# Recurrence of an RWKV-7 mixer: the next pair's scores around this pair's chunk terms, a second matrix tile, turns and head sums inside the levels, one key scaling on GpSimd

## The chip, the cores and the metric

The kernel runs on one core of one Trainium2 chip. The metric is the device time of one execution in microseconds (us), the median of three runs for the kernel before.

## The reference, cut to what matters

The program is two transformer-like blocks on 512 tokens of width 1024, all in float32. The change lies in the second block's RWKV-7 time mixer. For each of 8 heads (64 channels each) and each token it computes

```
state = state * w_t + (state @ a_t) b_t^T + v_t k_t^T      # a = -kk, b = kk * a, decay w
y_t   = state @ r_t
```

and after it a group norm, a bonus `sum(r*k*r_k) * v` and a gate. Everything ahead of it (first block, attention, projections) and behind it (merge, convolutional feed-forward) is not touched.

## The kernel before, in words

**Chunks and pairs.** The recurrence is rewritten in chunks of 64 tokens (`C`), 8 chunks. Heads are taken two at a time: pair m = 0 to 3, 128 channels on 128 partitions. For a pair, keys and removal keys scaled by the running decay ("hats") are multiplied with each other per chunk and head (`rw_scores`, line 973), which gives small 64x64 matrices `mats`; a triangular system of 64x64 is inverted by doubling in levels k = 1 to 5; the inverse is applied (`ug`, line 1126), and the terms of each chunk follow (lines 1137 to 1152: the map of the state and the outputs it adds). After all four pairs a short walk over the 8 chunks (lines 1163 to 1189) chains them.

**Halves.** All eight 64x64 units of a pair are split into two halves of two token tiles each, `half` 0 and 1. Half 0 uses PSUM banks 4 and 5, half 1 banks 0 and 1 (`HALF_BANKS`), and banks 2 and 3 take their transposed copies (`TURN_BANKS`). So while half 0 waits for a copy, TensorE works on half 1.

**One pair on TensorE** (line 1085 on), in program order: wait for the five hats; scores of half 0; turns of the keys from channels to tokens by transposes (`rw_turn(m, 0)`, banks 6 and 7); scores of half 1; turn of the values (`rw_turn(m, 1)`) and of the removal keys (`rw_turn_a`); `level_start(0)`; the two sums over heads of the next pair (`head_sums`, lines 957 and 960: of the squared keys and of the bonus product); then the levels. A level is `level_x` of half 0, `level_dt` of half 1 of the level before, `level_x` of half 1, `level_d` 0, `level_dt` 0, `level_d` 1. The first has `level_start(1)` in it and after its `level_x` 1 `keyed_values` (line 1037) into banks 2 and 3, whose copy `akv_read` must be over before `level_dt`. Then come `ug` of both halves, the wait for their copies, and the chunk terms into banks 0 to 3.

**The other engines** follow the same order, each a fixed list with waits on semaphores. ScalarE (line 1609 on) copies the turned keys, `Dm` and half of the `DT` copies out of PSUM, takes the exponentials of the decays (`decays`), the norm of the keys (`key_norm`) and the key rates of the pair after next (`key_rates`), and copies `UG` and half of the chunk terms. VectorE (line 2190 on) masks the scores into `mats`, makes the level starts, adds the identity in `X`, makes the other `DT` copies, and prepares the next pair inside the levels: `sums_out`, `decay_sum` (a scan), `decayed` (two products, line 2147 and 2149, `MOD * INV` being the scaling of the keys), `removal`, then `replacement` and `keys`. It reads the other half of the chunk terms (lines 2231 and 2232). GpSimd (line 501 on) makes the level masks `OT` (line 509), one product of the next pair (`rate_over_decay`, line 492) and `fold_decay` (line 498).

**Order between pairs.** `mats` is one tile and the scores of pair m+1 share banks 0, 1, 4 and 5 with pair m, so pair m+1's scores stand behind pair m's chunk terms, half 1 also behind their reading. "Hats" counts five operations per pair.

## Time and profile before

| | us |
|---|---|
| median of 3 runs (lowest, highest) | 1942.52 (1942.04, 1943.04) |
| the profiled execution: its own time | 1942.0 |
| its span, first to last instruction | 1940.1 |
| scores of pair 0 to the next pair's scores | 1334.8 to 1363.4 |
| pair 1 | 1363.4 to 1391.25 |
| pair 2 | 1391.25 to 1419.3 |
| pair 3, to the last chunk term | 1419.3 to 1447.0 |

TensorE is busy 95% of the span, with weight loads of 75%, VectorE 40%, ScalarE 22%, GpSimd 65%. Two thirds of the program are large 128x512 products; the four pairs take 112 us of 1940, in thousands of 64x64 products. In a row of the timeline the first number is the start, the second how long the group lasts, and square brackets hold the idle time before it and what ended it. A product's recorded duration includes its passage through the array, so neighbouring rows overlap: what one group costs its engine is the distance from its start to the next start.

### The profile page before, as it was taken

To read this page: it belongs to the slowest core of one execution; us is meant where nothing else is said; L and a number is where in the kernel's file an instruction comes from. 1 tells how busy PE (TensorE), PEld (TensorE's weight loads), DVE (VectorE), ACT (ScalarE), POOL (GpSimd) and SP (SyncE) were. 2 spreads that over 40 slices of the span, in tenths; PEclk is the share of its full clock that TensorE was granted. 3 is DMA by queue.
4 is the path that set the end of the run, shared out by engine and by line. 5 is a ranking of instruction groups with operands and counts; after the bars stand their busy time and mean duration, and the time that the engine had idled before them with its cause. 6 is when DMAs were issued, how large, how long until landed. Compare 5 with 4: busy or idle time off the path is not lost.

```text
span 1940.1 us, 29759 instructions
## 1 busy us (share of the span) xinstructions
PE 1843.9 (95%) x11700; PEld 1463.9 (75%) x11700; DVE 774.7 (40%) x1348; ACT 436.0 (22%) x885; POOL 1269.6 (65%) x621
## 2 busy tenths in 40 slices
PE   7999999988779999999899999998889999999998
PEld 5888888856557888888577787667776878888887
DVE  4333361164654333311322434515755445555301
ACT  3000001033522000000212245644534122112000
POOL 6888888844075888888566643242465867777773
PEclk8999999989989999999899999999999999999999
DMA  4222333221021222233332352140014322222331
GB/s 156 94 93 96 103 91 98 83 92 66 12 87 59 94 96 97 93 99 96 137 131 76 121 180 70 55 153 34 4 42 196 98 87 96 93 95 92 101 92 60
DMA packets 58779, 180.32 MB, mean 93 GB/s; under 512 B 6931, under 2 KB 13843, under 8 KB 58172
## 3 DMA queue, kind: packets, MB, share of 16 engines
q1 hardware_dynamic: 49132, 165.83, 25.4%
q10 hardware_dynamic: 9552, 13.13, 2.0%
q8 instruction: 72, 1.18, 0.2%
q14 instruction: 23, 0.19, 0.0%
HBM read 165.81 MB, written 13.13 MB: 92 GB/s over the span
## 4 chain that ended last, share of the span: by engine, by line
PE 89%; DVE 7%; ACT 2%; issue 1%; DMA 0%; SPq 0%; DVEq 0%; ACTq 0%
PE bank L546 26%; PE bank L547 25%; PE bank L548 25%; PE bank L596 1%; PE bank L893 1%; PE bank L922 1%; PE bank L866 1%; DVE h_lo L1714 1%; PE bank L828 1%; DVE xT L1761 1%; DVE tmp L1758 1%; PE bank L1081 1%; PE bank L1053 0%; PE bank L647 0%; DMA prm<-params_dram 0%
## 5 line engine op out<-in xcount | busy, mean ns | idle before, releaser
L454 POOL TENSOR_TENSOR w_hi<-w_raw,one 128x1024 fp32r<-128x1024 f32 (+1 forms) x279 | 524.5, 1880 | 537.9 <-PE bank L548 527.5
L456 POOL TENSOR_TENSOR w_lo<-w_raw,w_hi 128x1024 fp32r<-128x1024 f32 (+1 forms) x279 | 691.8, 2480 | 21.9
L546 PE MATMUL bank<-h_hi,w_hi 128*128 128x512 f32 x1528 | 621.1, 406 | 26.8 <-DVE h_lo L1714 12.1
L547 PE MATMUL bank<-h_lo,w_hi 128*128 128x512 f32 x1528 | 598.9, 392 | 0.0
L548 PE MATMUL bank<-h_hi,w_lo 128*128 128x512 f32 x1528 | 598.3, 392 | 0.0
L546 PEld LDWEIGHTS bank<-h_hi,w_hi 128*128 128x128 f32 x1528 | 289.2, 189 | 109.8 <-issue 28.3
L547 PEld LDWEIGHTS bank<-h_lo,w_hi 128*128 128x128 f32 x1528 | 289.5, 189 | 68.0 <-issue 10.7
L548 PEld LDWEIGHTS bank<-h_hi,w_lo 128*128 128x128 f32 x1528 | 289.1, 189 | 61.2
L546 PE MATMUL bank<-a_hi,w_hi 128*128 128x512 f32 x528 | 205.4, 389 | 0.0
L547 PE MATMUL bank<-a_lo,w_hi 128*128 128x512 f32 x528 | 205.4, 389 | 0.0
L548 PE MATMUL bank<-a_hi,w_lo 128*128 128x512 f32 x528 | 205.4, 389 | 0.0
L1294 ACT ACTIVATE tmp<-tmp 128x512 f32<-128x512 f32 x44 | 27.9, 633 | 426.6 <-DVE tmp L1725 426.6
L546 PEld LDWEIGHTS bank<-a_hi,w_hi 128*128 128x128 f32 x528 | 99.1, 188 | 20.6
L548 PEld LDWEIGHTS bank<-a_hi,w_lo 128*128 128x128 f32 x528 | 99.1, 188 | 20.6
L547 PEld LDWEIGHTS bank<-a_lo,w_hi 128*128 128x128 f32 x528 | 99.1, 188 | 20.5
L1751 DVE TENSOR_TENSOR acc<-acc,sq 128x512 f32<-128x512 f32 x16 | 29.6, 1848 | 189.3 <-ACT sq L1303 189.3
L1725 DVE TENSOR_TENSOR tmp<-bank,rstd 128x512 f32<-128x512 f32 x44 | 30.4, 692 | 132.4 <-PE bank L548 123.8
L1733 DVE TENSOR_TENSOR a_hi<-tmp,bank 128x512 f32 x44 | 30.3, 688 | 132.2 <-PE bank L548 132.2
L509 POOL TENSOR_TENSOR OT<-mats,rcs 128x256 f32<-128x256 f32 x40 | 32.5, 827 | 69.6 <-DVE mats L2195 61.9
L1687 ACT ACTIVATE tmp<-bank,prm 128x512 f32<-128x512 f32 x44 | 34.3, 780 | 147.8 <-DVE bank L2326 147.8
L1728 DVE TENSOR_TENSOR tmp<-tmp,rstd 128x512 f32<-128x512 f32 x44 | 47.1, 1071 | 31.4 <-ACT tmp L1294 31.4
L596 PE MATMUL bank<-sq,cst 128*128 128x512 f32 x96 | 55.1, 679 | 3.8 <-ACT sq L1268 3.8
(347 smaller groups left out, 1944.9 us busy)
## 6 DMA issues: line engine op xcount, KB each, us to landing
w_raw<-w_ffn_gu_dram SPq DMA_DIRECT2D x88, 512.0 KB, 3.4
w_raw<-w_conv_up_dram SPq DMA_DIRECT2D x44, 512.0 KB, 3.5
w_raw<-w_ffn_down_dram SPq DMA_DIRECT2D x32, 448.0 KB, 3.2
w_raw<-w_ffn_down_dram SPq DMA_DIRECT2D x16, 512.0 KB, 3.5
w_raw<-w_out_dram SPq DMA_DIRECT2D x16, 512.0 KB, 3.5
w_raw<-w_gates_dram SPq DMA_DIRECT2D x16, 512.0 KB, 3.5
w_raw<-w_rwkv_dram SPq DMA_DIRECT2D x14, 512.0 KB, 3.5
w_raw<-w_conv_down_dram SPq DMA_DIRECT2D x16, 448.0 KB, 3.3
```

The costliest lines, as they stand in the source:

```text
L454: nc.gpsimd.tensor_tensor(w_hi[:, s, 0:width], raw, one[:, 0:1].to_broadcast([P, width]), ALU.mult).then_inc(sem("w_rounded"), 1)
L456: nc.gpsimd.tensor_tensor(w_lo[:, s, 0:width], raw, w_hi[:, s, 0:width].bitcast(F32), ALU.subtract).then_inc(sem("w_split"), 1)
L509: nc.gpsimd.tensor_tensor(OT[:, k % 2, units_of(half), :] .rearrange("p (n e) t -> p n e t", e=2), mats[:, 2 * half:2 * half + 2, :, 0, :] ...
L546: nc.tensor.matmul(dst, hi, rhs_hi[:, k, :], start=start and k == k0, stop=False)
L547: nc.tensor.matmul(dst, hi, rhs_lo[:, k, :], start=False, stop=False)
L548: last = nc.tensor.matmul(dst, lo, rhs_hi[:, k, :], start=False, stop=stop and k == k1 - 1)
L596: nc.tensor.matmul(bank[b][:, :], ones, sq[:, k % 2, :], start=(k == 0), stop=(k == n - 1)).then_inc(sem(used), 1)
L1687: nc.scalar.activation(tmp[:, v, :], bank[2 * u + v][:, :], ACT.Identity, bias=bias, scale=w)\
L1725: nc.vector.tensor_tensor(tmp[:, u, :], bank[2 * u][:, :], rstd[:, :], ALU.mult)\
L1728: nc.vector.tensor_tensor(tmp[:, u, :], tmp[:, u, :], rstd[:, :], ALU.mult)\
L1733: nc.vector.tensor_tensor(hi, tmp[:, u, :], bank[2 * u + 1][:, :], ALU.mult)\
L1751: nc.vector.tensor_tensor(acc[:, :], acc[:, :], sq[:, m % 2, :], ALU.add).then_inc(sem(tag + "_acc"), 1)
```

## The change

The diff below is cut; names as above. `pe`, `act`, `dve`, `pool` are TensorE, ScalarE, VectorE and GpSimd.

```diff
+            odd_mats = in_h("mats1", [P, NT, 2, 4, C])
-        HALF_BANKS, TURN_BANKS = ((4, 5), (0, 1)), (2, 3)
+        HALF_BANKS, TURN_BANKS, SCORE_BANKS = ((4, 5), (0, 1)), (2, 3), ((4, 5), (6, 7))
-            mats = in_a("mats", [P, NT, 2, 4, C])
+            pair_mats = [in_a("mats", [P, NT, 2, 4, C]), odd_mats]
 # pool
+            def key_over_decay(m):
+                MOD = pair_sets[m % 2][1]
+                pool.wait_ge(*nth("decays", 2 * (m + 1)))
+                pool.wait_ge(*nth("rk_product", m + 1))
+                nc.gpsimd.tensor_tensor(MOD[:, :], MOD[:, :], INV[:, :], ALU.mult).then_inc(sem("hats"), 1)
                     if k == 4 and m < 3:
                         rate_over_decay(m + 1)
+                    if k == 5 and m < 3:
+                        key_over_decay(m + 1)
 # pe
             def keyed_values(m):
-                pe.wait_ge(*nth("rw_tok", 4 * m + 3))
-                pe.wait_ge(*nth("d_ready", 10 * m + 2))
+                pe.wait_ge(*nth("rw_tok", 4 * m + 4))
+                if m < 3:
+                    pe.wait_ge(*nth("bonus_done", m + 2))
...                                              # its banks are 6 and 7, not 2 and 3
             def level_dt(m, k, half):
-                if k == 1:
-                    pe.wait_ge(*nth("akv_read", m + 1))
-                elif k == 5:
+                if k == 5:
+            pe.wait_ge(*nth("hats", 5))
+            rw_scores(0, 0)
+            rw_turn(0, 0)
+            pe.wait_ge(*nth("rw_tok", 2))
+            rw_scores(0, 1)
             for m in range(4):
-                pe.wait_ge(*nth("hats", 5 * (m + 1)))
-                rw_scores(m, 0)
-                rw_turn(m, 0)
-                if m:
-                    pe.wait_ge(*nth("chunk_terms_read", m))
-                rw_scores(m, 1)
-                rw_turn(m, 1)
-                rw_turn_a(m)
                 if m:
                     pe.wait_ge(*nth("chunk_terms_copied", m))
                 level_start(m, 0)
-                if m < 3:
-                    pe.wait_ge(*nth("rw_tok", 4 * m + 4))
-                    head_sums(m + 1)
                 for k in range(1, 6):
                     level_x(m, k, 0)
                     if k > 1:
                         level_dt(m, k - 1, 1)
                     else:
+                        if m:
+                            pe.wait_ge(*nth("chunk_terms_read", m))
                         level_start(m, 1)
+                        rw_turn(m, 1)
                     level_x(m, k, 1)
                     if k == 1:
+                        rw_turn_a(m)
+                    elif k == 2 and m < 3:
+                        pe.wait_ge(*nth("rw_tok", 4 * m + 3))
+                        square_sum(m + 1)
+                    elif k == 3 and m < 3:
+                        pe.wait_ge(*nth("rw_tok", 4 * m + 4))
+                        bonus_sum(m + 1)
+                    elif k == 4:
                         keyed_values(m)
...
+                pe.wait_ge(*nth("akv_read", m + 1))
...                                              # ug of both halves
+                if m < 3:
+                    pe.wait_ge(*nth("hats", 5 * (m + 2)))
+                    pe.wait_ge(*nth("ug_read", 2 * m + 1))
+                    rw_scores(m + 1, 0)
+                    rw_turn(m + 1, 0)
                 pe.wait_ge(*nth("ug_read", 2 * m + 2))
...                                              # chunk terms of pair m
+                if m < 3:
+                    pe.wait_ge(*nth("rw_tok", 4 * m + 6))
+                    rw_scores(m + 1, 1)
 # act, inside the levels
-                    if k == 1 and m < 3:
-                        key_norm(m + 1)
+                    if k == 1:
+                        rw_turned(m, 2)
+                        rw_turned(m, 3)
                     elif k == 2 and m < 3:
                         decays(m + 1)
-                    elif k == 4 and m < 2:
-                        key_rates(m + 2)
+                    elif k == 3 and m < 3:
+                        key_norm(m + 1)
+                    elif k == 4:
+                        act.wait_ge(*nth("akv", m + 1))
+                        nc.scalar.activation(AtV[...], two_banks(6, 4 * C), ACT.Copy).then_inc(sem("akv_read"), 1)
+                        if m < 2:
+                            key_rates(m + 2)
...                                              # UG copies of both halves
+                if m < 3:
+                    rw_turned(m + 1, 0)
+                    rw_turned(m + 1, 1)
 # dve
-                nc.vector.tensor_tensor(MOD[:, :], MOD[:, :], INV[:, :], ALU.mult).then_inc(sem("hats"), 1)
+                if m == 0:
+                    nc.vector.tensor_tensor(MOD[:, :], MOD[:, :], INV[:, :], ALU.mult).then_inc(sem("hats"), 1)
+            masked_scores(0, 0)
+            masked_scores(0, 1)
             for m in range(4):
...                                              # the masking of both halves stood here
-                    if m < 3 and k < 5:
-                        (sums_out, decay_sum, decayed, removal)[k - 1](m + 1)
-                level_dt_out(m, 5)
+                    if m < 3 and k == 1:
+                        decay_sum(m + 1)
+                    elif m < 3 and k == 2:
+                        square_sum_out(m + 1)
+                    elif m < 3 and k == 3:
+                        decayed(m + 1)
+                        bonus_out(m + 1)
+                    elif m < 3 and k == 4:
+                        removal(m + 1)
                 if m < 3:
                     replacement(m + 1)
+                level_dt_out(m, 5)
                 if m < 2:
                     keys(m + 2)
+                if m < 3:
+                    masked_scores(m + 1, 0)
                 dve.wait_ge(*nth("chunk_terms", m + 1))
...                                              # the two readings of the chunk terms
+                if m < 3:
+                    masked_scores(m + 1, 1)
```

`masked_scores(m, half)` is the masking and level start that stood at the head of VectorE's loop, `square_sum` and `bonus_sum` are the two halves of `head_sums`, `square_sum_out` and `bonus_out` those of `sums_out`. `mats` of odd pairs lies in `odd_mats`, and scores of half 1 now go to banks 6 and 7.

## Rows read from the trace of the kernel before

**Rows 1.** The page's chain that ended last, shares of the span.
```profile
PE 89%; DVE 7%; ACT 2%; issue 1%; DMA 0%; SPq 0%; DVEq 0%; ACTq 0%
```

**Rows 2.** Windows, one row per pair: stretch, its us, busy us by engine, TensorE clock.
```profile
1334.80:1363.40 28.60, 24.13 (x874) 20.43 (x878) 20.57 (x36) 14.52 (x32) 9.95 (x11) 1.00 0.04 13
1363.40:1391.25 27.85, 23.87 (x899) 20.31 (x894) 20.41 (x36) 14.29 (x32) 11.60 (x13) 1.00 0.02 5
1391.25:1419.30 28.05, 23.89 (x892) 20.23 (x887) 18.96 (x34) 12.98 (x30) 11.60 (x13) 1.00 0.01 4
1419.30:1447.00 27.70, 23.66 (x891) 21.15 (x883) 12.41 (x25) 11.20 (x26) 20.59 (x18) 0.94 0.02 5
```

**Rows 3.** Waits in the four pairs: who for whom, total us, times, longest.
```profile
PE bank L1066 <- DVE X L2213: 3.7, 3, 1.2
PE bank L1081 <- ACT AtV L1621: 1.7, 4, 0.5
```

**Rows 4.** Timeline of TensorE, pair 2; the last row is pair 0's.
```profile
1391.25 0.40 PE L982 MATMUL bank<-AR,KK 64*64 64x128 f32 x8
...
1393.26 0.45 PE L982 MATMUL bank<-AR,KK 64*64 64x128 f32 x8
...
1394.88 1.15 PE L1008 MATMUL bank<-rcs,AR 64*64 64x64 f32 x32
...
1396.72 1.12 PE L957 MATMUL bank<-sq,rcs 128*128 128x512 f32 x2
...
1398.64 0.46 PE L1053 MATMUL bank<-Dm,OT 64*64 64x64 f32 x16
1398.92 0.34 PE L1020 MATMUL bank<-rcs,DT 64*64 64x64 f32 x6
...
1400.67 0.46 PE L1053 MATMUL bank<-Dm,OT 64*64 64x64 f32 x16 [0.88 <-ACT DT L1618]
...
1403.00 0.45 PE L1053 MATMUL bank<-Dm,OT 64*64 64x64 f32 x15
...
1414.05 1.36 PE L1126 MATMUL bank<-AtV,DT 64*64 64x128 f32 x32
1416.13 0.34 PE L1137 MATMUL bank<-mats,UG 64*64 64x64 f32 x8 [0.72 <-ACT UG L1644]
...
1347.29 0.45 PE L1053 MATMUL bank<-Dm,OT 64*64 64x64 f32 x15
```

**Rows 5.** Timeline of VectorE and ScalarE, start of pair 2.
```profile
1391.50 0.69 DVE L2231 TENSOR_TENSOR pin<-bank,AR 128x512 f32<-128x512 f32 x1 [2.34 <-PE bank L1152]
...
1392.82 1.29 DVE L2195 TENSOR_TENSOR mats<-bank,rstd 128x512 f32<-128x512 f32 x2
...
1394.60 0.83 DVE L2207 TENSOR_TENSOR DT<-X,rcs 128x256 f32<-128x256 f32 x1
...
1391.99 0.59 ACT L1651 ACTIVATE pin<-bank 128x512 f32<-128x512 f32 x1
```

**Rows 6.** One product alone (line view), and two on both engines at once.
```profile
L2128 DVE TENSOR_TENSOR MOD<-MOD,pin x4: 693/693/693, 1312.4 to 1387.7; 128x512 f32<-128x512 f32 x4
...
1408.18 1.76 DVE L2149 TENSOR_TENSOR MOD<-MOD,CUM 128x512 f32<-128x512 f32 x1
...
1407.62 1.78 POOL L492 TENSOR_TENSOR sig<-sig,CUM 128x512 f32<-128x512 f32 x1 [2.48 <-ACT CUM L1574]
```

**Rows 7.** Timeline of TensorE in pair 3, then two windows there.
```profile
1427.97 0.65 PE L1053 MATMUL bank<-Dm,OT 64*64 64x64 f32 x16 [0.88 <-ACT DT L1618]
...
1431.36 0.30 PE L1053 MATMUL bank<-Dm,OT 64*64 64x64 f32 x2
...
1441.12 0.33 PE L1126 MATMUL bank<-AtV,DT 64*64 64x128 f32 x2
...
1424.80:1428.00 3.20, 1.43 (x54) 1.19 (x53) 1.68 (x3) 1.32 (x4) 3.13 (x4) 1.00 0.02 5
1428.00:1431.40 3.40, 3.13 (x97) 2.94 (x100) 0.42 (x1) 0.94 (x3) 2.44 (x4) 0.51 0.00 0
```

More of the change, by code:

```diff
@@ L510, in _ @@
                                                 .rearrange("p (n e) t -> p n e t", e=2),
-                                                mats[:, 2 * half:2 * half + 2, :, 0, :],
+                                                pair_mats[m % 2][:, 2 * half:2 * half + 2, :, 0, :],
                                                 level[k].unsqueeze(1).unsqueeze(1).to_broadcast([P, 2, 2, C]),
@@ L952, in lora, with square_sum @@
                     .then_inc(sem("lora"), 1)
[L954 removed]
+            def square_sum(m):
                 pe.wait_ge(*nth("rw_square", m + 1))
@@ L958, in head_sums, with bonus_sum @@
                     .then_inc(sem("rw_head_sum"), 1)
+            def bonus_sum(m):
                 pe.wait_ge(*nth("rk_product", m + 1))
@@ L969, in _ @@
             fill(1)
-            head_sums(0)
+            square_sum(0)
+            bonus_sum(0)
             fill(3)
@@ L981, in rw_scores @@
                             rows, tok = half_rows(e), slice(n * P + c * C, n * P + c * C + C)
-                            last = nc.tensor.matmul(bank[HALF_BANKS[half][e]][half_rows(c), at], src[rows, tok],
+                            last = nc.tensor.matmul(bank[SCORE_BANKS[half][e]][half_rows(c), at], src[rows, tok],
                                                     AR[rows, n, :, half_rows(c)], start=True, stop=True,
@@ L1036, in keyed_values @@
                         rows = half_rows(c)
-                        last = nc.tensor.matmul(bank[2 + c][half_rows(e), n * C:n * C + C], mats[rows, n, e, 2, :],
+                        last = nc.tensor.matmul(bank[6 + c][half_rows(e), n * C:n * C + C], mats[rows, n, e, 2, :],
                                                 Vt[rows, n, half_rows(e)], start=True, stop=True,
@@ L1608, in _ @@
             by_bank = lambda x: x.rearrange("p (n b) t -> p b n t", b=2)
+            rw_turned(0, 0)
+            rw_turned(0, 1)
             for m in range(4):
                 AtV = pair_sets[m % 2][3]
-                for i in range(4):
-                    rw_turned(m, i)
                 for half in range(2):
@@ L2119, in decay_sum @@
                 dve.wait_ge(*nth("lora_read", m + 1))
+                if m:
+                    dve.wait_ge(*nth("hats", 5 * m))
                 nc.vector.tensor_tensor_scan(CUM[:, :], reset[:, :], SG[m], 0.0, ALU.mult, ALU.add)\
@@ L2166, in replacement @@
                 nc.vector.tensor_copy(PC[:, m, 1:], decay[:, 0:NCH - 1, C]).then_inc(sem("hats"), 1)
-                dve.wait_ge(*nth("hats", 5 * (m + 1)))
             def level_dt_out(m, k):
@@ L2183, in _ @@
             decayed(0)
-            sums_out(0)
+            square_sum_out(0)
+            bonus_out(0)
             removal(0)
@@ L2189, in _, with masked_scores @@
             dve.wait_ge(*nth("fill_late", 16 * LATE))
+            def masked_scores(m, half):
+                mats = pair_mats[m % 2]
+                dve.wait_ge(*nth("rw_scores", 2 * m + half + 1))
+                for e in range(2):
+                    last = nc.vector.tensor_tensor(mats[:, 2 * half:2 * half + 2, e, :, :],
+                                                   bank[SCORE_BANKS[half][e]][:, :]
+                                                   .rearrange("p (n j t) -> p n j t", n=2, j=4),
+                                                   mask4[:, :].rearrange("p (n j t) -> p n j t", n=2, j=4),
+                                                   ALU.mult)
+                last.then_inc(sem("mats_ready"), 1)
+                dve.wait_ge(*nth("mats_ready", 2 * m + half + 1))
+                to = X[:, units_of(half), :]
+                link(nc.vector.tensor_tensor(to.rearrange("p (n e) t -> p n e t", e=2),
+                                             mats[:, 2 * half:2 * half + 2, :, 0, :],
+                                             level[0].unsqueeze(1).unsqueeze(1).to_broadcast([P, 2, 2, C]),
+                                             ALU.mult))
+                nc.vector.tensor_tensor(DT[:, units_of(half), :], to,
+                                        eye2.unsqueeze(1).to_broadcast([P, 4, C]), ALU.add)\
+                    .then_inc(sem("level_start"), 1)
```

36 lines of the change are left out of this document (9 added, 27 removed).

## The prediction

> **What bounds the kernel now.** I read the page's chain first: TensorE holds 89% of it, so this is a TensorE-bound program [rows 1], and the change touches only the four pairs of the recurrence. Then one window per pair [rows 2]: each takes about 28 us, TensorE works 23.7 to 24.1 of them, and no other engine is busy for more than 20.6. Nothing is saturated but TensorE, and it idles about 4 us per pair. All the change can win by filling is those 4 us, some 16 us of 1942 over four pairs, 0.8%; it removes no product of TensorE's and adds none. Third, where the idle time lies: in the waits, TensorE stands three times for `X` of VectorE (up to 1.2 us each, total 3.7, one in each of pairs 0 to 2, where VectorE scales the keys ahead of `X` in level 4) and 0.5 for the copy of the keyed values [rows 3]. In the timeline of pair 2 there is 0.88 ahead of level 1's second half and 0.72 for the copy of `UG` [rows 4]. These four make 3.3 of the 4.2 us that pair 2 idles.
>
> I cut a pair into three parts and measure each from pair 2, T being the moment when the last chunk term of the pair before has left TensorE (1391.25): head, from T to level 2 (1403.00), 11.75 us; levels, from there to `ug` (1414.05), 11.05; tail, from there to the next T (1419.30), 5.25 [rows 2, 4]. They add to 28.05.
>
> **The head after the change.** Scores of half 0 and the key turns have moved out of it: 1391.25 to 1393.26, 2.0 us [rows 4]. So have the head sums, 1396.72 to 1398.64, 1.9 us, and the keyed values. But now the head is no longer filled by them and VectorE sets it. It reads the chunk terms from T+0.25 and is free for the second half's masking at T+1.57; masking, `X` and `DT` take from 1392.82 to 1395.43, 2.6 us [rows 5], and half 1's masking must stand behind the reading. So `level_start(1)` can go at T+4.25. From a level start to the `level_x` that reads its copies, pair 2 shows 1398.92 to 1400.67, 1.75 us [rows 4], so `level_x` 1 of half 1 goes at T+6.0. Half 0 is earlier: ScalarE's copies of the chunk terms end at T+1.33 [rows 5], so its start goes at T+1.5, its `level_x` at T+3.25. The turn of the values lies in the gap before T+6.0 and costs nothing; without that cover it would cost 0.6. From `level_x` of half 1 to level 2 pair 2 takes 1400.67 to 1403.00, 2.33 [rows 4]; the keyed values (about 0.5) and the wait for their copy (0.5) go out, and the turn of the removal keys (1.0; 1.15 with its last product's passage) comes in: 2.35. Level 2 begins at T+8.35 instead of T+11.75, a gain of 3.4. What is late next there is VectorE, not TensorE.
>
> **The levels after.** The four levels 2 to 5 take 11.05 in pair 2. Pair 3, which prepares no next pair, shows what they cost TensorE with nothing in the way: 1431.36 to 1441.12, 9.76 [rows 7]. Now the two head sums (1.9) and the keyed values (0.5) stand in them, all on TensorE's own list: 9.76 + 1.9 + 0.5 = 12.2. The 1.2 us wait for `X` is gone with the key scaling, and the `keyed_values` wait too. The decays' copies, the key norm and the key rates on ScalarE lie beside TensorE's extra products, except in level 5 of pairs 0 and 1, where the copy of the keyed values stands ahead of the key rates and `DT` of level 5 behind both.
>
> What the trace doesn't show is GpSimd's key scaling at that place. It follows the masks of level 5 and falls on VectorE's `removal`, whose products read two tiles of SBUF. The nearest rows: a 128x512 product alone takes VectorE 0.69; beside GpSimd's product of the same size (1.78) it takes 1.76 [rows 6], 1.07 more. So the price lies between nothing (they miss each other, or the key rates cover it) and 1.05 on `X` of level 5. I take 0.3, nearer to the lower end because in pairs 0 and 1 the key rates hide about 0.45 of it and VectorE may be through its first product before GpSimd begins. GpSimd's own time is slack: it ends some 3 us before the hats are wanted. Levels: 12.5, a loss of 1.45.
>
> On this pair of engines the Trainium skill (GPSIMD Engine Reference, Specifications) says that GpSimd's SBUF interfaces are shared with VectorE and that instructions with two SBUF inputs contend. The row agrees: 0.69 against 1.76. By this rule alone, with every two-input product of `removal` met, the sum would take the upper end, 0.75 more in each of three pairs.
>
> **The tail after.** `ug` 0 needs its copy; today both copies are over 2.08 after `ug` begins (1414.05 to 1416.13) [rows 4], and one is some 0.6 sooner. The next pair's scores and turns, 2.0 us, go in at +1.5 and the chunk terms at +3.5 instead of +2.08: a loss of 1.4, of which the 0.72 wait has paid its part. The hats are there: `replacement` now stands before the last `DT` copy, whose product takes longer than it. The masking of half 0 (2.6) lies beside the chunk terms (3.2, 1416.13 to 1419.30). If that cover failed, it would delay the reading at T and cost what sticks out. Queued on ScalarE behind its wait for the key turns are only the chunk copies, which are wanted later.
>
> **The sum.** Pair 0: its head is short on other grounds (1334.8 to 1347.29 is 12.5 us [rows 2, 4], its scores cannot be earlier, VectorE masks both halves in a row in both kernels); only the head sums go from the second half's way, between 0 and 1 us, I take 0.5. So -0.5 + 1.45 + 1.4 = +2.35. Pairs 1 and 2: -3.4 + 1.45 + 1.4 = -0.55 each. Pair 3: no next pair, so no head sums, no key scaling and the old tail. Its head goes from 12.06 (1419.30 to 1431.36) to 8.35, -3.7, the levels gain the keyed values, +0.5: -3.2 [rows 2, 7]. Together 2.35 - 1.1 - 3.2 = -1.95.
>
> **The clock.** In pair 3 the granted clock falls from 2.4 to 1.2 GHz for 3.4 us, after a stretch in which TensorE was busy 1.43 of 3.2 us; what pair 2 does in 2.33 us (1400.67 to 1403.00) takes 3.39 there (1427.97 to 1431.36), 1.06 more [rows 4, 7]. My head has full clock. But the new head is thin in every pair: level start, `level_x`, level start and value turn, about 2.9 us of products in the 5.1 between the scores and T+6.0, near to the ratio at which it fell in pair 3; the head sums that fill this stretch now in pairs 0 to 2 are gone. The price lies between 0 and four falls at 1.06 to 1.5 (the stretch behind now holds the 1.0 us turn of the removal keys, which would double). I count one fall, 1.06, as the trace before has one. Net: -1.95 + 1.06 = -0.9.
>
> The profiled execution took 1942.0 with a span of 1940.1, half a us below the median 1942.52. 1942.0 - 0.9 = 1941.1, and with that half 1941.6. This kernel's comparison can tell 0.2%, 3.9 us, from no change: faster means below 1938.6, slower above 1946.4.
>
> **Rivals.**
> - *Slower: the clock falls in every pair.* Place: T+1 to T+6 of each head. For it: the row of pair 3, and that the change thins the very stretch. Against it: dense products (chunk terms, scores) stand just before, and 2.9 of 5.1 is more than 1.43 of 3.2. Price: 1.5 in each of four pairs, 6.0 instead of 1.06: -1.95 + 6.0 = +4.05, 1946.6. It decides from four falls on; with two or three the result is within 0.2%.
> - *Faster: my chains overstate the waits.* If the halves interleave so that a pair idles 2 us instead of 3.5 (TensorE 23.9 of 25.9), pairs 1 and 2 give -2 each and pair 0 +0.8, with pair 3's -3.2: -6.4, less one fall, 1937.2. For it: the four waits named above are all addressed. Against it: the level start behind VectorE is a new wait of some 2.3 us in each head that nothing fills.
> - *VectorE becomes the bound.* It is busy 20.4 of 28 us already [rows 2], and the reading of the chunk terms comes behind the masking of half 0. If its work shifts each T-chain by 1 us in pairs 1 to 3, +3: 1944.6. For it: nothing on VectorE overtakes. Against it: the key scaling leaves it, 0.7 to 1.8 us [rows 6].
> - *The change doesn't do what it says*, since the scores must still wait for the hats or the turned keys: the tail grows by 1 us in three pairs, also 1944.6.
>
> On the first: the Trainium skill (TensorE: Matmul & The Clock Gate, What's actually happening) says that the default is the throttled clock and activity releases it. By that rule thin heads pay in each pair, the first rival's 1946.6; pair 3's row agrees, while pairs 0 to 2, whose idle gaps lie apart, kept full clock [rows 2].
>
> **How the numbers follow.** Forecast 0.46; clock rival 0.16; faster rival 0.24; VectorE bound 0.09; hats 0.05. The first holds to within 3 us, 1938.6 to 1944.6. Faster by over 0.2%: the faster rival and a little of the forecast, 0.26. Slower: the clock rival and an edge of the others, 0.18. Within: 0.56. The range adds the faster rival's point and the slower's with 1 us: 1937.0 to 1947.5; bounds of the unknown costs alone, -1.95 - 0.9 at no collision and no fall and -1.95 + 2.25 + 6.0 at both in full, give 1939.7 to 1948.8.
>
> **What would show it.** Right: the first `level_x` of half 1 about 6 us behind the last chunk term, with TensorE idle ahead of it for VectorE's `DT`; no wait for `X` in level 4; levels 2 to 5 at 12.2 to 12.8 in pairs 0 to 2; scores about 1.5 behind `ug`; pair 0 longer than before, pairs 1 and 2 27 to 28 us, pair 3 nearer to 24.5. VectorE's product at GpSimd's key scaling of 1.7 us or 0.7 settles the collision. Wrong: pairs 1 and 2 under 26.3 or over 28.5, or a granted clock below 1 in more than two heads.

## The result, and the profile after

| | before | after |
|---|---|---|
| median of ten runs each, us (lowest, highest) | 1942.66 (1939.51, 1944.7) | 1948.99 (1945.19, 1951.6) |
| ratio after to before, 95% interval | | 1.0032 [1.0024, 1.0041] |
| profiled execution: its time, its span | 1942.0, 1940.1 | 1945.74, 1943.9 |
| the four pairs, in the profiled execution | 112.20 | 119.65 |

The change made the kernel 6.3 us slower. The forecast was 1941.6, the range ended at 1947.5. The four pairs alone are 7.45 us longer; in this one execution pair 0 began at 1331.65 instead of 1334.80, ahead of anything that was changed, which is why the spans lie only 3.8 apart. I therefore compare the pairs from here on.

The page of the kernel after; its chain answers to [rows 1]:

```profile
PE 89%; DVE 8%; ACT 2%; issue 1%; DMA 0%; SPq 0%; DVEq 0%; ACTq 0%
```

The chain says nothing: a change of 0.3% doesn't show in whole per cents. Windows of the kernel after, one per pair, columns as in [rows 2], and the four pairs as one window:

```profile
1331.65:1363.13 31.48, 27.54 (x921) 23.16 (x924) 22.63 (x39) 15.72 (x34) 11.71 (x13) 0.95 0.04 12
1363.13:1393.15 30.02, 25.36 (x891) 21.78 (x886) 20.20 (x35) 14.18 (x32) 13.28 (x14) 0.94 0.02 4
1393.15:1423.15 30.00, 25.46 (x898) 21.72 (x894) 18.92 (x33) 13.09 (x30) 13.27 (x14) 0.94 0.01 4
1423.15:1451.30 28.15, 22.62 (x851) 20.50 (x840) 9.91 (x21) 9.81 (x24) 20.77 (x17) 0.88 0.02 4
...
1331.65:1451.30 119.65, 100.98 (x3516) 87.16 (x3516) 71.66 (x128) 52.80 (x120) 59.03 (x58) 0.93 0.02 6
```

The same one window of the kernel before:

```profile
1334.80:1447.00 112.20, 95.55 (x3516) 82.11 (x3516) 72.35 (x131) 52.99 (x120) 53.75 (x55) 0.98 0.02 7
```

Read the first two numbers and the clock. Both have 3516 matmul records: the work is the same. TensorE was busy 5.4 us longer for it (95.55 to 100.98), the clock being 0.93 instead of 0.98, and idle 2.0 longer (16.65 to 18.67). Every pair has a clock below 1 now, where before only pair 3 had [rows 2].

What it idled for, from the waits of TensorE in that window (who waits for whom, us in total, times, longest); it answers to [rows 3]:

```profile
PE bank L1031 <- DVE DT L2244: 4.0, 4, 1.3
PE bank L993 <- issue: 3.5, 3, 1.4
PE bank L1065 <- ACT DT L1642: 3.5, 4, 0.9
PE bank L1091 <- issue: 2.5, 3, 1.1
PE bank L1078 <- issue: 1.5, 2, 1.2
...
PE bank L1091 <- DVE X L2255: 0.5, 1, 0.5
```

The 3.7 us of waits for `X` in front of `level_d` and the 1.7 for the keyed values are gone, as intended. In their place stands "issue", a wait for nothing the profile shows: eleven idle places, 8.35 us in the four pairs by the timeline, where the kernel before has three, 1.11 us. The waits for data fell from 15.5 to 10.3 us, and the new ones ate all of that and 2 us more.

The timeline of TensorE in pair 2, which answers to [rows 4], T being 1393.15:

```profile
1393.15 0.31 PE L993 MATMUL bank<-AR,KK 64*64 64x128 f32 x2
...
1395.18 0.33 PE L993 MATMUL bank<-AR,MOD 64*64 64x128 f32 x3 [1.43 <-issue]
...
1397.56 0.46 PE L1065 MATMUL bank<-Dm,OT 64*64 64x64 f32 x16 [0.87 <-ACT DT L1642]
1398.94 0.39 PE L1031 MATMUL bank<-rcs,DT 64*64 64x64 f32 x6 [0.91 <-DVE DT L2244]
...
1400.72 0.71 PE L1065 MATMUL bank<-Dm,OT 64*64 64x64 f32 x16
1401.18 1.84 PE L1019 MATMUL bank<-rcs,AR 64*64 64x64 f32 x30
...
1404.15 0.46 PE L1065 MATMUL bank<-Dm,OT 64*64 64x64 f32 x16
...
1413.81 0.39 PE L1091 MATMUL bank<-DT,X 64*64 64x64 f32 x7 [1.14 <-issue]
```

Head 11.0 us (1393.15 to 1404.15), levels 12.4 (to `ug` at 1416.54), tail 6.6 (to 1423.15). VectorE in the same head answers to [rows 5]:

```profile
1394.08 0.68 DVE L2283 TENSOR_TENSOR pin<-bank,rcs 128x512 f32<-128x512 f32 x1
1396.18 1.29 DVE L2232 TENSOR_TENSOR mats<-bank,rstd 128x512 f32<-128x512 f32 x2 [1.42 <-PE bank L993]
```

It has read the chunk terms at 1394.76, as forecast (T+1.6), and then waits 1.42 us for scores whose instructions had not come. And four windows of the head and one behind it, for the clock:

```profile
1393.40:1396.70 3.30, 1.86 (x66) 1.48 (x56) 1.81 (x3) 1.08 (x2) 0.00 (x0) 1.00 0.03 5
1396.70:1400.10 3.40, 1.63 (x51) 1.48 (x52) 2.36 (x5) 0.84 (x3) 2.55 (x4) 0.99 0.00 0
1400.00:1403.40 3.40, 3.39 (x70) 3.02 (x70) 1.91 (x2) 0.58 (x2) 3.40 (x5) 0.50 0.02 5
1403.40:1407.00 3.60, 3.60 (x120) 2.76 (x116) 1.87 (x5) 2.19 (x6) 2.06 (x3) 1.00 0.02 5
1427.30:1434.20 6.90, 6.00 (x126) 5.39 (x123) 1.91 (x4) 0.81 (x3) 5.50 (x7) 0.51 0.01 2
```

After a half idle head TensorE was granted 1.2 instead of 2.4 GHz for 3.4 us (clock 0.50 in the third row), and just then a dense part stands (busy 3.39 of 3.40). Pair 3 has twice as long a fall, pairs 0 and 1 one of 3.4 each (1338.6 and 1369.3).

Where do the instructions come from? The DMA lines of the page cut to 12 us of the kernel after, in 40 slices of 0.3 us, show one kind of traffic only:

```profile
GB/s 0 0 55 0 0 0 0 0 0 0 0 0 0 0 0 55 0 0 0 0 0 0 0 0 0 0 0 55 0 0 0 0 0 0 0 0 0 0 0 0
q8 instruction: 3, 0.05, 2.0%
```

and windows of one us around the stall, 1392 to 1396 (last number GB/s):

```profile
1392.00:1393.00 1.00, 1.00 (x84) 1.00 (x78) 0.00 (x0) 0.00 (x0) 0.00 (x0) 1.00 0.08 16
1393.00:1394.00 1.00, 0.75 (x39) 0.51 (x28) 0.53 (x1) 0.53 (x2) 0.00 (x0) 1.00 0.00 0
1394.00:1395.00 1.00, 0.00 (x0) 0.00 (x0) 0.76 (x2) 0.56 (x2) 0.00 (x0) 1.00 0.00 0
1395.00:1396.00 1.00, 0.82 (x33) 0.82 (x34) 0.00 (x0) 0.00 (x0) 0.00 (x0) 1.00 0.00 0
```

A transfer of 16 KB starts every 3.6 to 3.9 us and takes 1.3 us (2.0% of 16 engines' 12 us for three of them). The one that starts at 1392.5 is over at 1393.8, and the stall ends 1.4 us later, at 1395.18. This led to theory A of the experiments: TensorE's own program arrives in pieces, and dense stretches of small products outrun it. The places of the stalls say so too. Windows from one stall's end to the next, the matmul records in brackets behind TensorE's busy time:

```profile
1391.44:1395.17 3.73, 2.30 (x128) 2.06 (x128) 1.43 (x3) 1.08 (x2) 0.00 (x0) 1.00 0.02 4
1413.80:1424.87 11.07, 9.75 (x380) 8.48 (x380) 7.14 (x14) 4.90 (x10) 0.97 (x1) 1.00 0.02 4
1439.03:1442.88 3.85, 2.66 (x127) 2.54 (x127) 1.23 (x3) 1.17 (x4) 3.77 (x2) 1.00 0.02 4
```

A record has a weight load beside it, so 128 records are 256 instructions, 16 KB. Of the ten distances in the changed kernel eight are 1, 2, 3 or 4 times 125 to 128 records, and the other two (106 and 146) make two such pieces together. Theory B was the first rival of the forecast, the clock alone.

### The profile page after: what moved, and what is told of

The parts are those of the page before. It is cut to its first block, busy times and chain, and to the rows that moved or that the text cites. A ratio compares the mean times of both kernels' runs of the same rounds, so it can differ in the third digit from the quotient of the medians.

```text
span 1943.9 us, 29772 instructions
## 1 busy us (share of the span) xinstructions
PE 1844.5 (95%) x11700; PEld 1465.0 (75%) x11700; DVE 775.0 (40%) x1345; ACT 435.6 (22%) x885; POOL 1273.3 (66%) x624
## 4 chain that ended last, share of the span: by engine, by line
PE 89%; DVE 8%; ACT 2%; issue 1%; DMA 0%; SPq 0%; DVEq 0%; ACTq 0%
PE bank L555 25%; PE bank L557 25%; PE bank L556 25%; PE bank L902 1%; PE bank L931 1%; DVE h_lo L1745 1%; PE bank L875 1%; PE bank L605 1%; DVE xT L1792 1%; DVE tmp L1789 1%; PE bank L837 1%; PE bank L1091 1%; PE bank L1065 0%; PE bank L1078 0%; PE bank L993 0%
## 5 line engine op out<-in xcount | busy, mean ns | idle before, releaser
L555 PE MATMUL bank<-h_hi,w_hi 128*128 128x512 f32 x1528 | 617.4, 404 | 27.4 <-DVE h_lo L1745 12.6
```

The source lines that it names most:

```text
L555: nc.tensor.matmul(dst, hi, rhs_hi[:, k, :], start=start and k == k0, stop=False)
```

## The experiments

Eighteen kernels ran in five sets. Each is compared with the kernel before on the same chip, by ratio, but for `e8_supply`, which ran once for its trace. "Stalls" are TensorE's idle places marked "issue" in the four pairs.

**First set.** Fillers against the clock, more instructions, and one part alone.

`e1_warm`, the changed kernel with

```diff
+def warm(b, n): n times matmul(bank[b][:, 0:256], ident, cst)      # 4 instructions each
                 level_start(m, 0)
+                warm(3, 2)
                     level_x(m, k, 0)          # k == 1: + warm(3, 2) behind it
                         rw_turn(m, 1)         # + warm(7, 1) behind it
```

> The changed kernel with five filler products per pair (identity times 256 constant columns, into a free bank, read by nobody) in the idle gaps of the head: two behind level_start(0), two behind the first level_x, one behind the turn of the values. Only 20 instructions per pair. Clock theory (the granted clock falls to 1.2 GHz in each head because the gaps are idle, 1.07 us per pair from level_x of half 1 to level 2, more in pair 3): clock 1.0 in all four heads, that stretch back from 3.4 to 2.4 us, pairs 1 to 3 shorter by 1 to 2 us each, in all 4 to 6 us under the changed kernel, 1943 to 1945. Instruction theory (TensorE runs out of instructions, stalls of 1.0 to 1.5 us put down to issue in the second scores and in level 4): clock may stay up, but pair 1 stays at 29 to 30 us since the stalls remain, gain under 2 us.

Measured: 1948.56, 1.0037 [1.0022, 1.0051]. No fall of the clock is left in the four pairs, and they still take 119.05 us; 7.5 us of stalls remain. But the five fillers per pair raise TensorE's busy time from 101.0 to 105.0 us, so this kernel alone can't tell what the clock is worth.

`e2_pad` (32 products of 8 columns, 128 instructions, ahead of pair 0) and `e3_tiny` (16 of them, 64 instructions, behind `level_x(m, 1, 0)` in every pair).

> The changed kernel with 32 tiny products (128 instructions, about 0.5 us of TensorE) once, ahead of pair 0's scores, so that everything behind lies 128 instructions later in the stream, half of a 16 KB piece. Instruction theory: the stalls put down to issue stand at other products (not in the 9th record of the second scores nor the 7th of level 4's dt), their sum of 8 us in the recurrence changes by 1 to 4 us either way. Clock theory, or stalls tied to a wait of those products: stalls at the same products, time equal to the changed kernel plus 0.5.

> The changed kernel with 16 tiny products (64x64 by 8 columns, read by nobody) per pair in the idle gap behind the first level_x: 64 more instructions per pair, but only some 0.5 us of TensorE, which fits into the idle 0.9 us. Instruction theory (a piece of 256 instructions can't be had faster than every 3.6 us or so): each pair 0.3 to 0.9 us longer, 1 to 3.5 us over the changed kernel. Clock theory: no change, or up to 2 us faster where the clock stays up. Neither: no change.

Measured: 1951.68, 1.0055 [1.0041, 1.0070], and 1955.19, 1.0068 [1.0054, 1.0083]. I read `e3_tiny` as support at first; its trace takes that back:

```profile
1344.32 3.15 PE L1111 MATMUL bank<-rcs 64*64 64x8 f32 x31
```

The 16 products, all on one quadrant, cost 2.9 us of TensorE there at half clock (to the next start, 1347.23), so the 6 us say nothing about instructions. The 32 of `e2_pad` took 3.6 us (1334.27 to 1337.91). By their times both are inconclusive. The trace of `e2_pad`, though, answers the first half of its expectation. Its waits of TensorE:

```profile
PE bank L1065 <- issue: 5.3, 7, 1.1
```

Seven of its ten stalls stand in `level_x` (L1065), where the changed kernel has none, and none in the second half's scores, and they lie 125 or 126 records apart, or two or five times that (250 to 254, 632). With the program shifted by half a piece the stalls moved to other products, as theory A had it.

`e4_keys`, the kernel before with GpSimd scaling the keys alone (`key_over_decay` behind the masks of level 5, as in the diff of the change).

> The kernel before with one part of the change alone: GpSimd scales the keys (behind its level 5 masks), VectorE doesn't. Prediction's theory: the 1.23 us wait for X in level 4 of pairs 0 to 2 goes, less what the collision with removal costs (0 to 1.05 on X of level 5): -0.5 to -3.6 us against before, 1939 to 1942. Rival: the wait comes back whole at level 5 or at the hats, no gain; or slower by up to 1 us per pair because the hats are late, since the scores follow the chunk terms at once.

Measured: 1940.73, 0.9994 [0.9985, 1.0003], no difference, and the trace shows why. Waits of TensorE in its four pairs, to be held against [rows 3]:

```profile
PE bank L1089 <- issue: 3.4, 3, 1.5
...
PE bank L1074 <- issue: 2.0, 2, 1.1
...
PE bank L1089 <- DVE X L2223: 0.2, 1, 0.2
```

The waits for `X`, 4.6 us over all lines, fell to 0.2, and the stalls for instructions rose from 1.1 to 7.6 (7.9 in an expectation further down is a slip). Removing the wait bought nothing: TensorE arrives at the same levels earlier and stands there for its program, again 125 to 127 records apart or a multiple of that. The clock never falls in its pairs, and they take 113.75 us.

**Second set.** Far fewer instructions for nearly the same work. `few` merges products in `level_x`, `level_d` and `level_dt`. One stationary then serves two units, so the second unit gets a wrong inverse: these kernels (and `e11_few_warm`) leave out part of the computation and serve for timing alone.

```diff
-for i in range(2): for c, e in DIAGONALS:
-    matmul(out[.., i*C:i*C+C], OT[rows, k % 2, 2*n+e, :], Dm[rows, 2*n+e, :])
+for c, e in DIAGONALS:      # one stationary for two units, 128 columns
+    matmul(out[.., 0:2*C], OT[rows, k % 2, u, :], Dm[rows, u:u+3:2, :])
```

> The changed kernel, in which level_x, level_d and level_dt issue one product of 128 columns for every two of 64 (one stationary for both, so the inverse is wrong): 448 fewer instructions per pair on TensorE of some 1850, nearly the same time in the array (0.26 us becomes 0.22 per call). Theory A (instruction supply: TensorE's program arrives in pieces of 256 instructions, one in 3.5 to 3.9 us at best, and a pair of the changed kernel needs 7.2 of them): the stalls without a releaser, 8.4 us in the changed kernel, fall under 2, and the time falls by 6 to 10, to 1939 to 1943. Theory B (only the clock costs, four falls): the calls get 28 x 0.04 = 1.1 us per pair shorter at most, 1944.5 or above, and the clock falls as before.

> The same edit in the kernel before. Theory A: that kernel has few stalls without a releaser (1.1 to 2 us) and waits 3.7 us for X, so it gains less than the changed one: 1 to 5 us, 1937 to 1941, and the distance between the two kernels, +6.3, shrinks to between -2 and +3. Theory B: both gain alike and the distance stays at +5 to +7.

Measured: the changed kernel so cut 1940.93, 0.9985 [0.9976, 0.9994]; the kernel before so cut 1943.15, 0.9999 [0.9990, 1.0007]. The first gained 8 us, the second nothing, below its expected gain. So the distance between the orders turned from +6.3 to -2.2. That the +6.3 vanished is far beyond the noise; that it became negative is hardly so, as the two intervals touch. Windows of the four pairs, changed kernel cut, then with the two fillers of a later run:

```profile
1334.39:1446.55 112.16, 96.58 (x2620) 78.26 (x2620) 70.87 (x128) 52.98 (x120) 55.97 (x57) 0.95 0.02 6
```

```profile
1335.52:1444.25 108.73, 97.46 (x2636) 76.83 (x2636) 70.16 (x128) 52.91 (x120) 56.27 (x57) 1.00 0.02 6
```

Stalls for instructions fell from 8.35 to 2.25 us in it, and three falls of the clock stayed. That the kernel before gained nothing is partly open: it kept its waits for `X` (4.9 us in all), and its stalls were 4.2 instead of 1.1, three of 1.1 to 1.4 in or just behind the chunk terms, which were not merged.

`e7_late`, the changed kernel with the next pair's scores and key turns (and ScalarE's copies and VectorE's masking of them) behind the chunk terms again:

```diff
-                if m < 3:      # between ug and the chunk terms
-                    rw_scores(m + 1, 0); rw_turn(m + 1, 0)
...
                 last.then_inc(sem("chunk_terms"), 1)
                 if m < 3:
+                    rw_scores(m + 1, 0); rw_turn(m + 1, 0)
                     rw_scores(m + 1, 1)
```

> The changed kernel with the next pair's scores and key turns behind this pair's chunk terms again (their copies and maskings too); turns of values and removal keys, head sums, keyed values and the key scaling stay where the change put them. Theory A: chunk terms and scores are then one dense stretch, the supply runs out in it as before; the head grows by the 2.0 us of scores that stood in the tail, and by the maskings: 1946 to 1951. Rival C (it is the scores around the chunk terms that cost): back to 1940 to 1943.

Measured: 1948.66, 1.0029 [1.0016, 1.0042], and 119.14 us for the four pairs. To take back the scores around the chunk terms, the title of the change, gives nothing back. One fall of the clock is left there and 6.9 us of stalls; the waits for data went from 10.3 to 15.8.

`e8_supply`, the disputed cost by itself: 360 products of 64 columns, then 240 of 128, on four quadrants.

> The kernel before with 360 products of 64 x 64 and then 240 of 64 x 128 (on an unused bank, nothing to wait for) ahead of pair 0: 1440 and 960 instructions. Theory A: the first stock goes at 16 to 18 ns a record, then stalls of about 1 us stand at every 256 instructions, so that the first block takes 3.5 to 3.9 us per 256 instructions behind its start, some 15 to 20 us in all, against 720 x 0.016 = 11.5 us without a limit; the second takes 27 ns a record, 256 instructions in 3.5 us, and shows few stalls. Theory B: 11.5 us and no stall in either.

The timeline of TensorE there (one row for each run of records without a stall):

```profile
1334.21 2.78 PE L1093 MATMUL bank<-cst,rcs 64*64 64x64 f32 x173 [0.69 <-ACT late_stage L1454]
1338.56 2.09 PE L1093 MATMUL bank<-cst,rcs 64*64 64x64 f32 x128 [1.57 <-issue]
1342.01 2.09 PE L1093 MATMUL bank<-cst,rcs 64*64 64x64 f32 x128 [1.36 <-issue]
1345.47 2.09 PE L1093 MATMUL bank<-cst,rcs 64*64 64x64 f32 x128 [1.36 <-issue]
1349.47 2.09 PE L1093 MATMUL bank<-cst,rcs 64*64 64x64 f32 x128 [1.91 <-issue]
1353.20 3.31 PE L1093 MATMUL bank<-cst,rcs 64*64 64x64 f32 x128 [1.64 <-issue]
1356.92 11.23 PE L1093 MATMUL bank<-cst,rcs 64*64 64x128 f32 x386 [0.41 <-issue]
```

and its instruction traffic from 1338 to 1352, slices of 0.35 us:

```profile
GB/s 0 0 0 0 47 0 0 0 0 0 0 0 0 0 47 0 0 0 0 0 0 0 0 0 47 0 0 0 0 0 0 0 0 0 0 47 0 0 0 0
...
q8 instruction: 4, 0.07, 2.0%
```

This is the clearest view of the case. A product in float32 is two matmul records and two weight loads, four instructions. Exactly 128 records, 256 instructions, run in 2.09 us, and then TensorE stands 1.36 to 1.91; one 16 KB piece in 3.45 us twice, then in 4.00, 3.73 and 3.72. (The row at 1353.20 holds the change of width: 35 narrow records and 93 wide ones.) Products of 128 columns take 10.93 us for 386 records, 28 ns each, about the pace of the supply (3.45 to 4.00 us for 128 records, 27 to 31 ns each), and show no stall inside. So in a long row a 64-column product, 16 ns a record by itself, costs as much as one of twice the width. The Trainium skill (Runtime: NRT & Kernel Launch, Instruction fetch mechanics) says that TensorE's program is refilled in 16 KiB blocks of 256 instructions and that crossing one is mostly hidden; the size agrees, "mostly hidden" doesn't hold here, with 1.36 to 1.91 us at each of them.

**Third set.**

`e9_starts` (the kernel before with the keys on GpSimd) and `e10_starts_after` (the changed kernel), both with `level_start`'s copies merged:

```diff
-for i in range(2): for c, e in DIAGONALS:
-    matmul(out[.., i*C:i*C+C], eye2[rows, :], DT[rows, 2*n+e, :])
+for c, e in DIAGONALS:
+    matmul(out[.., 0:2*C], eye2[rows, :], DT[rows, u:u+3:2, :])
```

> The kernel before with GpSimd scaling the keys, and level_start's copies through the identity as products of 128 columns, one for two of 64 (same result, 16 products or 32 instructions fewer per pair, of some 1800). With the key scaling alone that kernel stalled 7.9 us for instructions and was no faster than before. Theory A (instruction supply, 256 instructions in 3.45 us): 32 x 3.45 / 256 = 0.4 us per pair, 1.7 us in all below the kernel with the keys alone (0.9994 of before), so 0.998 to 0.999 of before, if every pair is bound by the supply; theory B (supply plays no part): what TensorE saves in the array, 0.1 us per pair, 0.999 to 1.0.

> The changed kernel with the same edit. Theory A: 1.5 to 2 us below the changed kernel, 1946.5 to 1947.5. Theory B: at most 0.5 below it, 1948.5.

Measured: 1944.9, 1.0010 [1.0001, 1.0020], and 1951.86, 1.0054 [1.0038, 1.0070]. Both miss, on the wrong side: 32 instructions fewer per pair, and some 3 to 4 us slower than without the edit, though the intervals with and without it nearly meet or overlap a little. The trace of the second has 12.0 us of stalls instead of 8.35. The mean rate would have it the other way; I took it that where the ends of the pieces fall must count too, which the fourth set tries.

`e11_few_warm`, the merged changed kernel with two fillers (`warm(3, 1)` behind `level_start(m, 0)` and behind the first `level_x`).

> The changed kernel with products merged in the levels (448 instructions fewer per pair, inverse wrong, 1940.9 us) and two filler products of 256 columns per pair in the idle places of the head (behind level_start 0 and behind the first level_x, where TensorE waits 0.9 and 0.7 us for copies). The kernel without the fillers fell to 1.2 GHz in three heads. If the clock costs 1.1 to 1.5 us for each fall of 3.4 us, as the trace of the changed kernel suggests, and the fillers keep it up: 3 to 4 us less, 1937 to 1938.5. If the falls stay or their time lies in waits anyway: 1940 to 1942.

Measured: 1937.15, 0.9973 [0.9963, 0.9982], as expected. Its window is the second above: clock 1.00, 3.4 us less than the first (3.8 by the medians, some 2.3 by the ratios). With instructions at hand the clock costs about what it seems to, and a head that keeps it pays.

`e12_spread`, the scores of half 1 behind `level_start(m, 0)`:

```diff
-                    rw_scores(m + 1, 1)        # straight behind the chunk terms
...
                 level_start(m, 0)
+                if m: rw_scores(m, 1)
```

> The changed kernel with the scores of half 1 of the next pair behind level_start of half 0 instead of straight behind the chunk terms: 16 products of 128 columns (1.1 us) leave the dense stretch in which the instructions ran out and stand where TensorE waited for VectorE. VectorE's second masking waits for them (from T+2.7 instead of T+1.6), so level_start 1 can go at about T+5.3, where it stands at T+5.1 to 5.8 now. Theory A and the clock: the 1.0 to 1.4 us stall behind the chunk terms falls beside the wait for their copies, one to two clock falls go: 1 to 1.5 us per pair in three pairs, 1944 to 1946. If the head is set by VectorE alone: the masking starts 1.1 later in three pairs, 1950 to 1952.

Measured: 1951.11, 1.0045 [1.0031, 1.0059], the second of the two. TensorE's waits for VectorE's `DT` grew from 4.0 to 8.9 us; VectorE stood 1.97 us for the scores in a head where it stands 1.42 now.

**Fourth set, the position.** Fillers of 8 columns on four quadrants ahead of pair 0, which shift all that follows by 64 or 128 instructions:

```diff
+for i in range(16 or 32): c, e = DIAGONALS[i % 4]
+    matmul(bank[c][half_rows(e), 0:8], eye2[half_rows(c), :], eye2[half_rows(c), 0:8])
```

> The changed kernel with 16 products of 8 columns on four quadrants ahead of pair 0: 64 instructions more, about 0.5 us of TensorE, and every boundary of a piece of 256 instructions falls 64 instructions earlier in the recurrence. If position matters: the time moves by more than its 0.5 us, up to 3 us either way (1946 to 1952.5), and other stalls come and go in the trace. If it doesn't: 1949.5.

> The same with 32 products, 128 instructions, half a piece, about 1 us of TensorE. If position matters: off 1950 by up to 3 us, and differently than with 64. If it doesn't: 1950.

> The kernel before with the same 16 products, 64 instructions, ahead of pair 0. Its waits for X leave the supply time to catch up, so the theory says it depends less on position: 1943 with the 0.5 us of the products, within 1 us of that. If it moves as much as the changed kernel, part of the measured +6.3 is position.

> The kernel before with 32 products, 128 instructions. 1943.5, within 1 us, by the theory; 1946 or more if position matters for it too.

| shifted by | changed kernel | kernel before |
|---|---|---|
| 0 | 1.0032 [1.0024, 1.0041] | 1 |
| 64 | 1.0041 [1.0027, 1.0056] | 1.0023 [1.0013, 1.0032] |
| 128 | 1.0035 [1.0021, 1.0048] | 1.0016 [1.0006, 1.0025] |

The kernel before depends on the position, against my expectation: 64 instructions shift it up by 4.5 us, of which the products are 0.5, and the stalls go from 1.1 to 9.2, while its waits for `X` fall from 4.6 to 1.3 us. Its place was a good one. The changed kernel at 128 has one fall of the clock instead of four and 11.4 us of stalls. The mean of the three rows is 1.0036 against 1.0013: some 4.5 us of the 6.3 belong to the order, some 2 to the position. Three positions of a period of 256 are few, so the split is rough; nothing here says what the two orders would do at the other places.

**Fifth set.** `e17_light_warm` is the changed kernel with the two fillers of `e11_few_warm`, `e18_keys_back` the changed kernel with VectorE scaling the keys (`if m == 0:` taken away, `key_over_decay` out).

> The changed kernel with the two filler products of 256 columns per pair in the head that took 3.8 us off the kernel with merged products (8 instructions per pair more). If clock and supply add: the four falls go, 3 to 4 us less than the changed kernel, 1945 to 1946, and 8 us of stalls for instructions remain. If the supply takes what the clock gives back (a faster head empties the stock sooner): 1947.5 to 1949.

> The changed kernel with VectorE scaling the keys of every pair again. If a wait for X and a stall for instructions exchange one for one, as the key scaling alone showed: 1948 to 1950, with some 3 us of waits for X and 3 to 4 us less of stalls. If the key scaling's collision with removal costs on its own (0.9 us on each of three pairs in the trace): 1946 to 1947.

Measured: 1948.13, 1.0025 [1.0016, 1.0035], and 1951.14, 1.0037 [1.0023, 1.0051]. One fall is left (pair 0), the clock over the four pairs is 0.99, and yet they take 120.20 us with 9.4 of stalls: the same two fillers that shortened the merged kernel's pairs by 3.4 us shorten nothing here. The medians say so less sharply (0.9 us, or 1.3 by the ratios, inside the intervals). The fillers cost TensorE time themselves (busy 101.7, as with the falls), and here, other than in the merged kernel, the idle time did not shrink for them (18.5 against 18.7). The second missed both expectations: no wait for `X` in front of the levels came back, the stalls stayed at 8.9, and it is no faster. The collision on VectorE costs nothing that can be seen; with intervals 3 us wide, and VectorE doing 0.7 us more per pair, a us or two could hide.

No kernel with the whole computation beats the kernel before: `e4_keys`, at 0.9994 [0.9985, 1.0003], is its equal.

## Why the prediction was wrong

**What failed.** Two terms, both in the head: the clock, counted as one fall at 1.06, and the supply of TensorE's program, which stood in no sum. The profiled executions, split by what TensorE did in the four pairs, in us ("half clock" is the time at 1.2 GHz):

| kernel | four pairs | busy | stalls | waits for data | half clock |
|---|---|---|---|---|---|
| before | 112.2 | 95.6 | 1.1 | 15.5 | 3.4 |
| `e4_keys` | 113.8 | 95.2 | 7.6 | 10.9 | 0 |
| changed | 119.7 | 101.0 | 8.4 | 10.3 | 17 |
| changed, shifted by 128 (`e14_after32`) | 118.5 | 97.2 | 11.4 | 9.9 | 3.4 |
| changed, two fillers (`e17_light_warm`) | 120.2 | 101.7 | 9.4 | 9.1 | 3.4 |
| before, merged (`e6_few_before`) | 113.4 | 92.6 | 4.2 | 16.6 | 0 |
| changed, merged (`e5_few_after`) | 112.2 | 96.6 | 2.3 | 13.3 | 10 |
| changed, merged, two fillers (`e11_few_warm`) | 108.7 | 97.5 | 1.7 | 9.6 | 0 |

The change did take 5.2 us of waits for data away. Stalls took 7.2 in their place, and the clock 5.4 of busy time. The two are no independent costs: the changed kernel shifted by 128 has one fall instead of four and no filler in its pairs, is busy 3.8 us less, and stalls 3.1 more. That a slower TensorE lets its program catch up is the plain reading; no run varies the clock alone. Only with both out of the way (the last row) is the changed order clearly ahead, by 4.6 us of `e6_few_before` in these single executions (0.9973 against 0.9999 by the ratios), at one position each.

**The instruction supply, which it did not have.** The forecast read idle time and busy time and took every wait removed as time won, less what the next wait for data costs. A pair is 1758 instructions (3516 + 3516 records in four), 6.9 pieces, 24 us at 3.45 each, under a pair's 28. On the mean there is room, in a dense stretch there is none: the chunk terms are 384 instructions in 2.85 us, 1.5 pieces. At its own place the kernel before stood for data while the supply caught up; `e4_keys` takes the wait for `X` out and gets the stalls, and shifted by 64 the wait gives way to stalls by itself. The three rows of "issue" in its timeline, 0.30 to 0.43 us, were there to see, and I did not ask about them. `e5_few_after` against `e6_few_before` has the forecast's sign and is near to its -0.9, but that proves little: the first holds three falls of the clock, and each stands at one position only, where positions alone moved the kernel before by 4.5.

**The head, 8.35 forecast.** The step that failed. The four heads took 12.6, 10.3, 11.0 and 11.4 us where the forecast has 12.0 and three times 8.35; that is 8.3 of the 9.4 by which the sum of -1.95 missed +7.45. All the falls of the clock and 3.5 of the stalls lie in them. Pair 2: `level_start(1)` at T+5.8 instead of 4.25, since the scores of half 1 ran into a stall of 1.43; `level_x` of half 1 at T+7.6 instead of 6.0; then 3.4 instead of 2.35 at half clock. 11.0 in all. What the step gained against 11.75 is 0.75 instead of 3.4.

**The clock, one fall at 1.06 forecast.** Four came, one of them double. TensorE's busy time for the same records is 95.20 us in `e4_keys`, which has no fall, and 100.98 in the changed kernel: 5.8 us. The first rival (a fall in every head, 6.0) was right in place and price, and its total, 1946.6, came within 2.4; but it rests on the same -1.95, which has no stalls in it, and so is partly luck. My case against it, that dense products stand ahead, failed: windows of 1.86 of 3.30 and 1.63 of 3.40 busy stand before the fall, more than the 1.43 of 3.2 of [rows 7]. But the falls are not the whole cause, nor can they be added: with none or one of them the changed kernel stays at 1948 (`e1_warm`, `e17_light_warm`, and without fillers in its pairs `e14_after32`). That a faster head only empties the stock sooner is argued from the table.

**The levels, 12.5 forecast.** The size is right, 12.5, 12.9, 12.4 in pairs 0 to 2, by two errors that cancel: stalls of 1.02 and 0.34 stand in pair 1's and 1.14 in pair 2's, and without them pair 2's would be 11.3, not 12.2. The 9.76 that I took for TensorE with nothing in the way held two stalls itself, 0.38 and 0.30 (1435.29 and 1438.68 in the trace before). Pair 3's take 10.8 instead of 10.26.

**The collision, 0.3 forecast.** It met `removal`'s first product in full; timelines of the kernel after in pair 2, VectorE and GpSimd, beside the 0.69 and 1.76 of [rows 6]:

```profile
1412.45 1.68 DVE L2192 SCALAR_TENSOR_TENSOR KK<-pin,prm,tmp 128x512 f32<-128x512 f32 x1 [0.16 <-ACT tmp L1605]
1414.16 0.69 DVE L2194 SCALAR_TENSOR_TENSOR AR<-KK,decay 128x512 f32<-128x512 f32 x1
```

```profile
1412.32 1.26 POOL L499 TENSOR_TENSOR MOD<-MOD,CUM 128x512 f32<-128x512 f32 x1
```

and VectorE at this product in the kernel before:

```profile
1410.86 0.90 DVE L2156 SCALAR_TENSOR_TENSOR KK<-pin,prm,tmp 128x512 f32<-128x512 f32 x1
```

1.68 against 0.90, 0.8 more, the upper end nearly. TensorE did not pay: VectorE is through at 1415.2 for the `X` of level 5, and TensorE came late from a stall at 1413.81.

**The tail, 6.65 forecast.** Right: 6.4, 6.8, 6.6; scores about 1.5 behind `ug`. **The pairs.** Pair 0 +2.9 (+2.35 forecast), pair 1 +2.2 and pair 2 +1.95 (-0.55), pair 3 +0.45 (-3.2). VectorE as the bound and a change that doesn't do what it says both fell away.

## What to carry to other kernels

Before a wait is filled on an engine with thousands of small instructions, count the instructions of the stretch against what its queue delivers, and treat each "issue" row as a question: a wait for data may be the time in which the program is fetched. Where pieces of the program are near the limit, a shift of 64 instructions can move the time by most of what the change under test does, so compare orders at several positions. And a head that is thinned ahead of the densest part can cost the clock of that part; fillers pay only if something else doesn't take the gain.

## What the hardware showed that I had not expected

- TensorE's program comes in 16 KB pieces of 256 instructions, one in 3.45 us at best in the dense row of `e8_supply` (2.09 us of work, 1.36 us idle), 13.5 ns per instruction; in the real kernels nearly all stalls stand whole pieces apart.
- A 64x64 float32 product in such a row costs 54 ns or more, a 64x128 one 57 ns, though the first takes 33 ns while instructions last.
- The granted clock fell to 1.2 GHz for 3.4 or 6.9 us behind stretches with 1.63 of 3.40 us busy, and the 3516 records took 100.98 us of busy time with 17 us at half clock, 95.20 with none (`e4_keys`).
- Products of 8 columns in a row on one quadrant took 0.11 us each (32 in 3.64 us, `e2_pad`), over three times a 64x64 one on four quadrants (33 ns).
- A 128x512 two-input product of VectorE took 1.68 us beside one of GpSimd of 1.26 us, and 0.90 in the kernel before, where it stood beside GpSimd's masks.
